# Strassen products for the up-projection of the second feed-forward net, with its down-projection as a pass of its own

## What is computed

```python
def conv_ffn(z, w_up, conv_w, conv_b, w_down):
    u = dwconv(z @ w_up, conv_w, conv_b, FFN_CONV // 2)   # 3 taps along the tokens, per column
    g, v = jnp.split(u, 2, axis=-1)
    return (jax.nn.silu(g) * v) @ w_down
...
xl = xl + mods[2] * yl
zl = modulate(rmsnorm(xl, norm2_g[l]), mods[3], mods[4])
xl = xl + mods[5] * conv_ffn(zl, ffn_w_up[l], ffn_conv_w[l], ffn_conv_b[l], ffn_w_down[l])
...
return rmsnorm(xl, final_g)
```

## Time and profile before

| | |
|---|---|
| median of 3 runs | 2935.9 us (2935.46 to 2936.94) |
| profiled execution, first to last instruction | 2934.1 us; the median of the runs lies 1.8 us above it |
| TensorE busy | 2889.2 us, 98% of the span |
| mean granted TensorE clock | 0.996 of full |
| VectorE, ScalarE, GpSimd busy | 1651.1, 1036.0, 462.8 us |
| second feed-forward net | from 2180 us to the end |

### The profile page before, as it was taken

One profiled execution on the slowest core, in us unless ns is written; L12 is line 12 of the kernel. 1 busy time (PEld: TensorE's weight loads), 2 busy tenths in 40 slices (PEclk: granted clock), 3 DMA queues, 4 the chain that ended last, 5 costly groups with the idle time before them and its releaser, 6 DMA issues. The chain is left out here.

```text
span 2934.1 us, 38695 instructions
## 1 busy us (share of the span) xinstructions
PE 2889.2 (98%) x15945; PEld 2408.5 (82%) x15945; DVE 1651.1 (56%) x2207; ACT 1036.0 (35%) x1279; POOL 462.8 (16%) x381
## 2 busy tenths in 40 slices
PE   8999999999999999999999999999999999999998
PEld 6888887888888888888887888888788888888887
DVE  7677666276666665566563154555545544545455
ACT  6676884142111221111142344444433222222223
POOL 3322231200000000000032444443310000000003
PEclk9999999999999999999999999999999999999999
DMA  9543434121211222222122433332511111111111
GB/s 335 146 120 115 111 91 169 40 62 61 65 59 57 86 79 72 77 68 79 44 79 90 141 89 90 99 85 67 179 57 51 47 47 50 47 47 44 51 47 69
DMA packets 266831, 250.27 MB, mean 85 GB/s; under 512 B 41747, under 2 KB 233586, under 8 KB 264608
## 3 DMA queue, kind: packets, MB, share of 16 engines
q1 hardware_dynamic: 251328, 193.45, 22.1%
q0 software_dynamic: 15296, 54.35, 5.9%
q10 hardware_dynamic: 32, 0.01, 0.0%
HBM read 214.03 MB, written 30.74 MB: 83 GB/s over the span
## 5 line engine op out<-in xcount | busy, mean ns | idle before, releaser
L726 PE MATMUL ps<-zH,wH 128*128 128x512 f32 (+1 forms) x2032 | 743.4, 366 | 2.0 <-DVEq L2519 2.0
L726 PE MATMUL ps<-zL,wH 128*128 128x512 f32 (+1 forms) x2032 | 741.9, 365 | 0.0
L726 PE MATMUL ps<-zH,wL 128*128 128x512 f32 (+1 forms) x2032 | 741.5, 365 | 0.0
L726 PEld LDWEIGHTS ps<-zH,wH 128*128 128x128 f32 x2032 | 383.4, 189 | 72.0 <-issue 7.8
L726 PEld LDWEIGHTS ps<-zH,wL 128*128 128x128 f32 x2032 | 383.2, 189 | 61.7
L726 PEld LDWEIGHTS ps<-zL,wH 128*128 128x128 f32 x2032 | 383.4, 189 | 61.3
L2538 DVE SCALAR_TENSOR_TENSOR res<-ps,mod,res 128x1024 f32<-128x1024 f32 x240 | 236.7, 1014 | 184.1 <-PE ps L726 172.1
L739 DVE SCALAR_TENSOR_TENSOR V<-ps,vec,V 128x1023 f32<-128x1023 f32 x126 | 122.2, 1011 | 283.1 <-ACT V L2390 282.4
L2360 ACT ACTIVATE wH<-wraw 128x1024 fp32r<-128x1024 f32 x129 | 133.7, 1051 | 389.5 <-PE ps L726 389.5
L726 PE MATMUL ps<-hH,wH 128*128 128x512 f32 (+1 forms) x700 | 259.7, 371 | 0.0
L726 PE MATMUL ps<-hL,wH 128*128 128x512 f32 (+1 forms) x700 | 258.4, 369 | 0.0
(11 more groups left out here) (347 smaller groups left out, 5146.7 us busy)
## 6 DMA issues: line engine op xcount, KB each, us to landing
wraw<-in_ffn_w_up_dram SPq DMA_DIRECT2D x88, 512.0 KB, 3.8
modw<-in_mod_w_dram POOLq DMA_DIRECT2D x40, 1024.0 KB, 5.7
wraw<-in_ffn_w_down_dram SPq DMA_DIRECT2D x44, 512.0 KB, 3.5
wraw<-in_na_w_in_dram SPq DMA_DIRECT2D x32, 512.0 KB, 4.0
bias<-scratch_bias SPq DMA_DIRECT2D x512, 32.0 KB, 1.8
v<-scratch_v SPq DMA_DIRECT2D x128, 64.0 KB, 2.0
wraw<-in_rg_w_in_dram SPq DMA_DIRECT2D x15, 512.0 KB, 5.6
scratch_xT<-res SPq DMA_DIRECT2D x8, 640.0 KB, 8.1
```

What stands on the lines that cost most here:

```text
L726: last = nc.tensor.matmul(ps[:, slot * SLOT + c:slot * SLOT + c + n], w(k), r(k)[:, c:c + n], start=(k == 0 and i == 0), stop=(k == K - 1 ...
```

## The change

Layer 1's `ffn` call is replaced by two parts, `up_last` and `down_last`; layer 0 keeps `ffn`.

**Strassen's form (in Winograd's variant).** For a pair i the weights are a 2 x 2 matrix of blocks: g and v columns by the lower four and the upper four row blocks of z. The two token halves make z a 2 x 2 matrix as well. Seven products replace the eight: of the weight blocks A11 (g, lower), A12 (g, upper), A22 (v, upper), and of four sums S1 = A21 + A22, S2 = S1 - A11, S3 = A11 - A21, S4 = A12 - S2, with the first-half z, its second half and four sums T1 to T4 of the z blocks, which are formed once. Each product is 4 row blocks x 3 matmuls. Pair 0 is multiplied in full, as before; pairs 1 to 21 take the form. Partial sums build up in PSUM: A12 adds onto A11's bank, S3 and A22 onto S2's, S4 onto S1's. The contents in between are needed too: `snap` (ACT) copies A11's, and DVE forms, in this order, s16 (snap + bank after S2), u3 (snap + bank after S3), c22 (u3 + bank after S1), c21 (snap + bank after A22), c12 (s16's + bank after S4). PE may start S3, A22 and S4 only when s16, u3 and c22 are formed. The four C blocks end in SBUF, in U; ACT makes the middle taps out of U into G and V, DVE adds the outer taps out of U.

**Who does the rest.** The split halves of A11, A12, A22 are made by ACT (high) and DVE (low); for S1 to S4, POOL makes the sum, ACT the high half, POOL the low one. They lie in eleven slots; a slot is free when the product that used it before is done (`slot_free`): the sum S1 of pair i+1 waits for A11 of pair i, S4's for A12.

**The down pass.** The gated row block V of each pair goes to DRAM (`scratch_h`), the residual too (`scratch_xT`). The pass takes b (token half) x q (two output blocks) x x (two h blocks), 88 chunks of 12 matmuls, each chunk with its own 256 KB of w_down, split anew (ACT high, POOL low, 11 chunks ahead). h is read back 256 KB at a time and split (ACT high, DVE low) in the first q of each b, into the space that z and T held. A whole output block adds up in PSUM over all 22 h blocks, in banks 0 to 2 in turn, and is added to the residual once. The last two output blocks of the second half (ITEMS) are cut into two pieces of 256 columns.

The core of the diff:

```diff
 def back(nc, m):
+    last_places(nc, m)
+    norm2, last = KeptPieces(nc, m, "n11", 1, 1, SEQ, m.zt), Pieces(nc, m, "fin", 1, None, SEQ, None, [(0, BANK), (BANK, BANK // 2), (BANK + BANK // 2, BANK // 2)])
     fin = final(nc, m, last)
-    up = ffn(nc, m, 1, SEQ, norm2, last, fin)
+    down = down_last(nc, m, last, fin)
+    up = up_last(nc, m, norm2, down)
     pr = project(nc, m, 1, m.t["na_w_out"][0], KD, SEQ, norm2, up)
...
+A11, S2, A12, S3, S1, A22, S4 = range(7)
+FIRST_ORDER = (A11, A12, S2, S1, S3, A22, S4)
...
+def up_last(nc, m, norm, nxt):
...
+    def slot_free(eng, s):
+        if s < KD:
+            eng.wait_ge(spilled, 16 * KD)
+            eng.wait_ge(norm.scaled, 2 * KD)
+        elif s < NS:
+            eng.wait_ge(first_done, 3)
+        else:
+            eng.wait_ge(prod_done, FILLED[s - NS])
...
+    def scalar(act):
...
+        for i in range(2, KF):
+            mid_g(i - 1)
+            snap(i)
+            silu(i - 1)
+            if i < KF - 1:
+                for x in (A11, A12, S2):
+                    high(i + 1, x)
...
+            c11(i)
+            if i < KF - 1:
+                for x in (S3, S1, A22, S4):
+                    high(i + 1, x)
...
+            mid_v(i)
...
+    def gpsimd(gp):
+        def sums(i):
...
+                add(S1, raw(i, "A21"), raw(i, A22), ALU.add)
+                add(S2, m.slotS[SLOT_AT[i, S1] % NS][:, :], raw(i, A11), ALU.subtract, S1)
+                add(S4, raw(i, A12), m.slotS[SLOT_AT[i, S2] % NS][:, :], ALU.subtract, S2)
+            add(S3, raw(i, A11), raw(i, "A21"), ALU.subtract)
...
+        for k in range(4):
+            gp.wait_ge(norm.scaled, KD + k + 1)
+            nc.gpsimd.tensor_tensor(m.T1S[:, k], half(Z("12", k)), half(Z("11", k)), ALU.subtract).then_inc(t_sum, 1)
+        for k in range(4):
...
+            nc.gpsimd.tensor_tensor(half(Z("11", k)), half(Z("22", k)), m.T1S[:, k], ALU.subtract).then_inc(t_sum, 1)
...
+            nc.gpsimd.tensor_tensor(Z("21", k), Z("21", k), Z("11", k), ALU.subtract).then_inc(t_sum, 1)
...
+        for i in range(2, KF):
+            sums(i)
+            for x in (S2, S3, S1, S4):
+                low(i, x)
...
+    def tensor(pe):
...
+            elif x in (S3, A22, S4):
+                pe.wait_ge(formed, FORMED.index((i, {S3: "s16", A22: "u3", S4: "c22"}[x])) + 1)
...
+        def t_ready(x):
+            if x in (S1, S2, S3, A22):
+                pe.wait_ge(t_low, {S1: 4, S2: 8, S3: 12, A22: 16}[x])
...
+    def vector(dve):
...
+        for i in range(2, KF):
+            c12(i - 1)
+            taps_v(i - 1)
+            taps_g(i - 1)
+            s16(i)
+            gated(i - 1)
+            if i < KF - 1:
+                low(i + 1, A11)
+                low(i + 1, A12)
...
+            u3(i)
...
+            c22(i)
+            if i < KF - 1:
+                low(i + 1, A22)
...
+            c21(i)
...
+def down_last(nc, m, norm, fin):
...
+    def sync(sp):
+        for j in range(EARLY_H, EARLY_H + 2):
+            load_h(sp, 0, j)
+        for n in range(4, 6):
+            load_w(sp, n)
+        for j in range(EARLY_H + 2, 12):
+            load_h(sp, 0, j)
+        part.prev.store(sp, KF - 1)
+        for n in range(6, NX):
+            load_w(sp, n)
+            for j in range(2 * n, 2 * n + 2):
+                load_h(sp, 0, j)
+            if n < 10:
+                q = n - 6
...
+                sp.dma_start(m.res_last[:, 2 * q:2 * q + 2, :], m.xT[2 * q:2 * q + 2, :, 0:SEQ].rearrange("k p n -> p k n")).then_inc(res_in[q], 16)
...
+    def vector(dve):
+        prev = part.prev
+        prev.c12(KF - 1)
+        low(dve, 0, 8)
+        low(dve, 0, 9)
+        prev.taps_v(KF - 1)
+        prev.taps_g(KF - 1)
+        low(dve, 0, 10)
+        low(dve, 0, 11)
+        prev.gated(KF - 1)
+        for j in range(12, KF):
+            low(dve, 0, j)
+        for n in range(CHUNKS):
+            if n + NX < CHUNKS:
+                b, q, x = split3(n + NX)
+                if (b, q) == (1, 0):
+                    for j in range(2 * x, 2 * x + 2):
+                        low(dve, 1, j)
+            if n < LAST_Q and n % NX == NX - 1:
+                add(dve, 2 * (n // NX))
+                add(dve, 2 * (n // NX) + 1)
+            fin.by_vector(dve, n)
```

More of the change, by code:

```diff
@@ L201, in build @@
     arena = pl.at
+    m.at = (modring_at, ring_at, z_at, arena)
     a = Plan(nc, arena)
@@ L638, in sums @@
             col = self.BANKS[c] * BANK + i
-            nc.tensor.matmul(m.ps[:, col:col + 1], m.acc[:, at + i * P:at + (i + 1) * P], m.ones[:, 0:1], start=True, stop=False)
+            nc.tensor.matmul(m.ps[:, col:col + 1], self.acc[:, at + i * P:at + (i + 1) * P], m.ones[:, 0:1], start=True, stop=False)
             ins = nc.tensor.matmul(m.ps[:, col:col + 1], sq[:, i * P:(i + 1) * P], m.ones[:, 0:1], start=False, stop=True)
@@ L3304, in attention, with number @@
     return part
+NS = 11
+A11, S2, A12, S3, S1, A22, S4 = range(7)
+FIRST_ORDER = (A11, A12, S2, S1, S3, A22, S4)
+NP_ALL = 7 * (KF - 1)
+def number(i, x):
+    return 7 * (i - 1) + (FIRST_ORDER.index(x) if i == 1 else x) + 1
+SLOT_AT = {(1, x): s for s, x in enumerate(FIRST_ORDER[2:])}
+for _i in range(2, KF):
+    for _x in range(7):
+        SLOT_AT[_i, _x] = len(SLOT_AT)
+FILLED = [number(*_key) for _key in SLOT_AT]
+N_UP = len(FILLED)
+NX = KF // 2
+CHUNKS = 2 * (KD // 2) * NX
+FILLED += [NP_ALL + _n + 1 for _n in range(CHUNKS)]
@@ L3316, in final @@
     BY_DVE = [(i, hf) for i in range(NT) for hf in range(2) if hf == 0 or i not in BY_ACT]
+    TILE = (0, 1, 0, 1, 0, 1, 2, 3)
+    BLOCK = CHUNKS // 2
+    SIX, SEVEN = KD - 2, KD - 1
     def rstd(i):
@@ L3322, in half, with tile_free, by_sync, send @@
         b = T_BANK[i % 2] + hf
-        return m.outT[:, i, hf * BANK:(hf + 1) * BANK], ps[:, b * BANK:(b + 1) * BANK], m.g_rows[:, hf * BANK:(hf + 1) * BANK]
+        return m.out_tiles[TILE[i]][:, hf * BANK:(hf + 1) * BANK], ps[:, b * BANK:(b + 1) * BANK], m.gain_rows[:, hf * BANK:(hf + 1) * BANK]
+    def tile_free(eng, i):
+        if 2 <= i < 6:
+            eng.wait_ge(stored, 64 * (i // 2))
     def load_gain(sp):
[L3326 to L3330, removed]
+        sp.dma_start(m.gain_rows[:, :], m.t["final_g"].unsqueeze(0).to_broadcast([P, D])).then_inc(gain_in, 16)
+    def by_sync(sp, n):
+        def send(i, hf):
             if (i, hf) in BY_DVE:
@@ L3341, in turn @@
         def turn(i):
-            pe.wait_ge(prev.item_added, KD * (PIECE_OF[i] + 1))
+            pe.wait_ge(prev.added, (KD, 2 * KD, 2 * KD + 2)[PIECE_OF[i]])
             if i >= 2:
```

826 lines of the change are left out of this document (781 added, 45 removed).

## The result

The changed kernel takes 2950.26 us (median; 2948.85 to 2950.66), the kernel before on the same chip 2936.42: ratio 1.0047, 95% interval 1.0035 to 1.0059. So it is slower, by about 14 us, more than the 0.2% that can be told from no change.

The account below looks back on a forecast made before the run. TensorE was taken as the bound, busy 2889.2 of 2934.1 us. Terms summed to +8.6, a span of 2942.7; the median lies 1.8 higher, so 2944 us against 2935.9; own range 2932 to 2956, whole range 2906 to 2966.

Parts of the forecast that it names:

- products removed, short matmuls: Second net: 252 fewer 512-column matmuls, -57.1 us; down-projection pieces cut to 256 columns, +0.95 us.
- idle of the old loop: Up-projection before the change: idle of 0.46 us per 200 us over some 650 us goes, -1.5 us.
- last stores: End of kernel: tiles 0 to 5 stored early, only four halves follow the last computation, -3.2 us.
- first pairs: Start of up-projection: S2, S3 and A22 wait for VectorE colliding with GpSimd, plus clock loss; +29.8 us.
- loop: Steady up-projection pairs: collisions make s16 and u3 late, a pair takes 20.3 us, not 19.04; 19 pairs, +24.3 us.
- hand-over: Up to down pass: chunks 5 to 10 wait for lows, the queued store and residual loads, plus clock loss; +15.1 us.
- chunk 44: Down pass: lows of h stand ahead of VectorE's addition that frees bank 0, so PE waits; +2.8 us.
- The loop keeps pace: Rival, chance 0.24: same collisions in the loop, but s16 and u3 in time; the 24.3 us goes, 2920 us.
- no collision: Rival, chance 0.10: VectorE and GpSimd operations do not collide at all; loop term 0, first pairs 17.6; 2906 us.
- POOL wins more turns: Rival, chance 0.12: GpSimd goes ahead of waiting VectorE more often, 2.8 us lost a pair; 2974 us.
- the hand-over hidden: Rival, chance 0.10: hand-over loads flow as the halves are freed; 8.6 us less, 2936 us, no change.
- The saving isn't there: Rival, chance 0.03: S1's moving operand, two runs of 256, costs two short matmuls each, 2.9 us in all; 2947 us.

Follow-up runs that it names:

- u3 ahead: Changed kernel with VectorE's loop reordered: s16 between two halves of the G taps, u3 right behind the gated product, ahead of all lows; 2922.5 us, 0.9953.
- the fill run: Changed kernel with GpSimd's sums and low parts in the up-projection of pairs 1 to 21 replaced by write-only fills; 2913.8 us, 0.9928.

## Right and wrong

The prediction was 2944 with slower at 0.50; the time is 2950. Its forecast case is the one that happened. Against the span, in us (the loop is 20 pairs by the c12 additions at 2256.82 and 2667.41, 410.6 for 380.8):

| term | predicted | in the trace |
|---|---|---|
| products removed, short matmuls | -56.15 | -56.15 by count |
| idle of the old loop | -1.5 | -7.7 |
| waits near the end | -2.6 | -3.2 (what the other rows leave) |
| last stores | -3.2 | -1.9 |
| first pairs | +29.8 | +31.2 |
| loop | +24.3 | +29.8 |
| hand-over | +15.1 | +15.7 |
| chunk 44 | +2.8 | +4.9 |
| sum | +8.6 | +12.6, the difference of the spans |

*Right:* where PE waits, for what, and nearly how long. S2, S3, A22: 8.39, 9.01, 4.00 predicted as 8.85, 9.1, 4.0. Chunk 6: 5.93 for 5.2. The next four: 5.6 for 7.6. Half speed behind chunk 6 cost 1.7 us for 1, and six restarts of PE, each a quarter of a microsecond, had not been priced. The 15.7 is of this execution; other traces with the same down pass are up to 2.4 us longer. The turn-taking tails of the earlier trace rows were good enough to place s16 and u3 within 0.1 us (8.1 and 14.1 us into the pair, as worked out).

*The loop, mis-sized.* "A pair takes 20.3 us": it takes 20.48. The two printed idles are 0.89 us of the 1.44 by which a pair is too long, the rest lies in PE's two restarts. That is 3.0 of the 5.5 us. "The last pair has no sums" was taken to mean no wait; there VectorE's four early lows of h stand ahead of u3 and meet GpSimd's weight lows (6.44 us for four), and A22 waits 2.22. With u3 ahead the last pair waits 1.1 in all.

*The first pairs, one row misread.* The prediction takes 2210.46 us for the end of the last matmul that is kept in front of S2. There are 120 of these, and the timeline of the kernel before has started 114 by then; the 120th ends its pitch at 2211.82. In the changed kernel it does so at 2213.25. So the first delay is 1.4 us and not 3.7.

*The clock, mis-sized.* "Half speed there costs 1.4 us", taken from one place after broken work, was 2.6 to 3.0 at each of the three: 8.3 us for 4.2. At chunk 44 it was left out: the wait of 3.45 us is followed by 1.5 us of half speed.

*The old loop's idle, mis-sized.* The 0.46 us idle in the earlier trace rows is only what a view of idle times shows. PE's timeline in the kernel before has the first matmul of two groups in a row at

```profile
2374.11 0.50 PE L2307 MATMUL ps<-hH,wH 128*128 128x512 f32 x1 [0.15 <-DVE G L2605]
...
2440.18 0.50 PE L2307 MATMUL ps<-hH,wH 128*128 128x512 f32 x1 [0.15 <-DVE G L2605]
```

that is 66.07 us for 288 matmuls, where 288 pitches are 65.29. Some five starts near the down items lie 0.28 to 0.54 us apart, and one alone shows an idle, of 0.15. Added up start by start from 2211.8 to 2888.5 us it makes 7.7 us. The change removed it, and 6.2 of it was not priced. Had the old loop run at its full pitch, the changed kernel would be 20 us behind and not 12.6.

*Luck.* That the total came within 6 us is in part luck. The loop (5.5), the clock in the first pairs (4.1) and chunk 44 (2.1) were priced too low, the old loop's idle (6.2) and the first delay (2.3) wrong the other way.

*The last stores:* from the start of the last addition to the end 9.3 us, 11.3 before; 1.9 saved, not 3.2.

*The rivals.* "The loop keeps pace" did not happen, but the run with u3 ahead shows how near it was: the same collisions and full pace, decided by three lows. Nearest to "no collision" is the fill run, 2914 where 2906 was worked out; GpSimd's T sums and its lows of w_down still read there. "POOL wins more turns" did not happen, a pair lost 1.44 us and not 2.8; nor was the hand-over hidden. "The saving isn't there" falls: with u3 ahead 84 matmuls take 19.04 us, 0.2267 each, S1's among them. The Trainium skill ("DMA: Bandwidth & Descriptors", Where 436 GB/s comes from) lets the DRAM side bind near 358 GB/s; the trace does not agree, from 2690.8 to 2705 us the hand-over moved 392 to 404 GB/s.

## What to carry over

When work is taken off the bounding engine and put on two others, lay those two side by side and look for instructions that both read SBUF: their durations from a trace in which each ran alone are too short, here by 0.9 us in 1.3. Then look at what the bounding engine waits for and issue it before all else that is merely due in the next round; here that was worth 28 of the loop's 30 us with nearly the same work on VectorE. Fast-algorithm savings of 57 us were worth 37 us net once this was done, and -14 before.
